# First units behind each norm multiply the residual before it is normed, with GpSimd taking part of the norm

## The reference

```
z = x @ w_in                                   # q, k, v of two attentions, forget logits, two gates
y = (sigmoid(ga) * (o_a @ w_pa) + sigmoid(gb) * (o_b @ w_pb)) @ w_o
x = layer_norm(ALPHA * x + y, ln1_g, ln1_b)    # norm 0 (layer 0), norm 2 (layer 1)
f = (gelu(conv3(x @ w_gate)) * (x @ w_up)) @ w_down
x = layer_norm(ALPHA * x + f, ln2_g, ln2_b)    # norm 1 (layer 0), norm 3 (layer 1, the output)

layer_norm(x, g, b) = (x - mean) * rsqrt(var + eps) * g + b
```

## Time and profile before

| | us |
|---|---|
| median of 3 runs (lowest, highest) | 960.76 (959.99, 963.42) |
| the profiled execution | 963.47 |
| its span, first to last instruction | 961.7 |
| TensorE busy in it | 936.3 (97%) |
| VectorE, ScalarE, GpSimd busy | 603.3, 506.5, 22.0 |

### The profile page before, as it was taken

The page is one execution under the profiler, slowest core; times in us unless marked ns, Lnnn a source line. Parts: engine busy times, 40 slices in busy tenths (PEclk is TensorE's granted clock), DMA queues, the critical chain, the costliest instruction groups (busy, mean ns, idle before and its releaser), DMA issues.

```text
span 961.7 us, 16399 instructions
## 1 busy us (share of the span) xinstructions
PE 936.3 (97%) x6488; PEld 900.9 (94%) x6488; DVE 603.3 (63%) x1211; ACT 506.5 (53%) x962; POOL 22.0 (2%) x39
## 2 busy tenths in 40 slices
PE   7999999998999999999899999999989999999996
PEld 5989999998999999999898999999989999999993
DVE  4675654678866666545587664548778566664545
ACT  4864454435855565533397544544467555653323
POOL 2000000000000000000000000000000000000000
PEclk9999999999999999999999999999989999999996
DMA  9744434554465554545735444355526555545511
GB/s 271 187 130 134 116 91 126 149 145 122 125 178 146 153 154 136 157 141 157 170 89 137 120 129 120 84 151 151 154 75 177 160 147 152 155 126 159 151 50 55
DMA packets 257765, 132.92 MB, mean 138 GB/s; under 512 B 22454, under 2 KB 254906, under 8 KB 257562
## 3 DMA queue, kind: packets, MB, share of 16 engines
q1 hardware_dynamic: 255930, 126.79, 47.4%
q0 software_dynamic: 1760, 5.09, 1.5%
HBM read 127.42 MB, written 4.57 MB: 137 GB/s over the span
## 4 chain that ended last, share of the span: by engine, by line
PE 97%; DVE 2%; ACT 1%; DMA 0%; issue 0%; SPq 0%; DVEq 0%
PE bank L625 28%; PE bank L626 27%; PE bank L627 27%; PE bank L695 3%; PE bank L840 2%; PE bank L641 1%; PE bank L647 1%; PE bank L644 1%; DVE roped_b L1394 1%; PE bank L799 1%; PE bank L795 1%; PE bank L792 1%; PE bank L814 1%; PE bank L696 1%; DMA gates<-in_x_sample 0%; DVE gates L1387 0%
## 5 line engine op out<-in xcount | busy, mean ns | idle before, releaser
L625 PE MATMUL bank<-act_hi,w_hi 128*128 128x320 f32 x1312 | 411.6, 314 | 0.0
L626 PE MATMUL bank<-act_lo,w_hi 128*128 128x320 f32 x1312 | 405.4, 309 | 0.0
L627 PE MATMUL bank<-act_hi,w_lo 128*128 128x320 f32 x1312 | 405.4, 309 | 0.0
L1161 DVE TENSOR_TENSOR w_lo<-raw,w_hi 128x1024 fp32r<-128x1024 f32 (+1 forms) x236 | 283.8, 1203 | 108.7 <-ACT w_hi L908 108.1
L908 ACT CAST w_hi<-raw 128x1024 fp32r<-128x1024 f32 (+1 forms) x236 | 244.2, 1035 | 154.7 <-PE bank L627 146.9
L625 PEld LDWEIGHTS bank<-act_hi,w_hi 128*128 128x128 f32 x1312 | 246.4, 188 | 2.7 <-DVE w_lo L1161 0.3
L626 PEld LDWEIGHTS bank<-act_lo,w_hi 128*128 128x128 f32 x1312 | 246.4, 188 | 0.2
L627 PEld LDWEIGHTS bank<-act_hi,w_lo 128*128 128x128 f32 x1312 | 246.3, 188 | 0.0
L625 PE MATMUL bank<-h_hi,w_hi 128*128 128x320 f32 x352 | 109.4, 311 | 0.0
L627 PE MATMUL bank<-h_hi,w_lo 128*128 128x320 f32 x352 | 108.8, 309 | 0.0
L626 PE MATMUL bank<-h_lo,w_hi 128*128 128x320 f32 x352 | 108.8, 309 | 0.0
(11 more groups left out here) (197 smaller groups left out, 999.3 us busy)
## 6 DMA issues: line engine op xcount, KB each, us to landing
raw<-in_w_in SPq DMA_DIRECT2D x62, 512.0 KB, 3.9
raw<-in_w_gate SPq DMA_DIRECT2D x44, 512.0 KB, 3.8
raw<-in_w_up SPq DMA_DIRECT2D x44, 512.0 KB, 4.3
raw<-in_w_down SPq DMA_DIRECT2D x32, 448.0 KB, 3.8
raw<-in_w_o SPq DMA_DIRECT2D x16, 512.0 KB, 4.1
raw<-in_w_down SPq DMA_DIRECT2D x16, 512.0 KB, 4.1
raw<-in_w_in SPq DMA_DIRECT2D x16, 256.0 KB, 5.2
raw<-in_w_pa SPq DMA_DIRECT2D x32, 128.0 KB, 2.8
```

What stands on the lines that cost most here:

```text
L625: pe.matmul(out, wh, hi[:, k0 + c, :], start=begin and c == 0, stop=False)
L626: pe.matmul(out, wh, lo[:, k0 + c, :], start=False, stop=False)
L627: mm = pe.matmul(out, wl, hi[:, k0 + c, :], start=False, stop=end and c == n_chunks - 1)
L1161: ve.tensor_tensor(w_lo[:, slot, :, :].rearrange("p c e -> p (c e)")[:, 0:w], raw[:, slot, 0:w], hi.bitcast(F32), ALU.subtract).then_inc(l ...
```

## The change

Norm of x times a weight is rewritten. With r the residual behind norm_tile (less its shift), W the weights and x = (r - mean) * root * g + b:

W x = root * (W (g r) - mean * (W g)) + W b

The first five units behind norms 0, 1 and 2 (FOLDED; gate 0, up 0, gate 1, up 1, gate 2, or forget, ka, va, qa 0, qa 1) multiply r_hi/r_lo, the two parts of g*r, with g and b as two more columns (322 in place of 320). r_hi is made by ACT and r_lo by DVE when a residual tile is ready. The statistics' matmuls stand within the first of these units. DVE then takes W g and W b from the bank (uv) and adds -mean * (W g) to the sum ("lift", into fixes, three buffers); GpSimd multiplies by the root and adds W b ("level"); the step behind reads fixes in place of the bank. GpSimd also centres all eight tiles and scales four of them. The three-unit group is gone: from the sixth unit on, units use act_hi/act_lo as before. The key transposes move to the units from ga 7 on, one tile behind each of five; cache and parameter transposes to units 2, 3 and 6 of their layer. The last norm is not folded, and there all centring comes behind the reciprocal. kT is split into kA and kB so that r_hi and r_lo have room.

```diff
-at_unit(TOP, "cache", 0)
-at_unit(TOP, "cache", 1)
-at_unit(TOP, "params", 0)
+at_unit(2, "cache", 0)
+at_unit(3, "cache", 1)
+at_unit(6, "params", 0)
...
-at_unit(NORM_UNITS[0], "keys", 0)
+for _k, _t in enumerate(KEY_TILES):
+    at_unit(AT[("ga", KC - 1)] + _k, "kv", _t)
...
+            def level(m, j):
+                at = FOLDED * m + j
+                pool.wait_ge(lifted, at + 1)
+                t = fixes[:, at % 3, :]
+                nc.gpsimd.tensor_tensor(t, t, rstd_of[m % 2], ALU.mult).then_inc(pool_chain, 1)
+                pool.wait_ge(pool_chain, at + 1)
+                nc.gpsimd.tensor_scalar(t, t, uv[:, j, 1:2], None, ALU.add).then_inc(levelled, 1)
+            def normalise(m):
...
+                passed(r_split, KC * (m + 1))
+                passed(mean_copied, m + 1)
+                for o in range(KC):
+                    nc.gpsimd.tensor_tensor(gates[:, o, :], gates[:, o, :], nmean_of[norm], ALU.add).then_inc(centred, 1)
+                passed(rstd_ready, m + 1)
+                level(m, 0)
+                for o in range(BY_POOL, KC):
+                    nc.gpsimd.tensor_tensor(gates[:, KC + o, :], gates[:, o, :], rstd_of[norm],
+                                            ALU.mult).then_inc(scaled_late, 1)
+                for j in range(1, FOLDED):
+                    level(m, j)
...
+                hi, lo, w = (r_hi[fold[0] % 2], r_lo[fold[0] % 2], WIDE) if fold else (act_hi, act_lo, TOK)
...
                 def ready(k):
-                    if fresh:
+                    if fold and fold[1] == 0:
+                        stats(fold[0], k)
+                        if k == 0:
+                            pe.wait_ge(edge_split, fold[0] + 1)
+                        pe.wait_ge(r_split, KC * fold[0] + k + 1)
+                    elif fresh:
                         pe.wait_ge(fresh[0], fresh[1](k))
...
+            def lift(l, u):
+                m, j = folding(l, u)
...
+                if j >= 3:
+                    dve.wait_ge(*consumed(l, u - 3))
+                dve.wait_ge(unit_used, SLOTS + unit_n(l, u + 1))
+                dve.wait_ge(mean_copied, m + 1)
+                b = bank[TILE[UNITS[u][:2]] % 4]
+                link(ve.tensor_copy(uv[:, j, :], b[:, TOK:WIDE]))
+                ve.scalar_tensor_tensor(fixes[:, at % 3, :], nmean_of[m % 2], uv[:, j, 0:1], b[:, 0:TOK], ALU.mult,
+                                        ALU.add).then_inc(lifted, 1)
...
+            def r_part(m, k):
...
+                dve.wait_ge(r_hi_made, KC * m + k + 1)
+                ve.scalar_tensor_tensor(r_lo[norm][:, k, 0:TOK], gates[:, k, :], par[:, g0 + k:g0 + k + 1],
+                                        r_hi[norm][:, k, 0:TOK].bitcast(F32), ALU.mult,
+                                        ALU.subtract).then_inc(r_split, 1)
...
+                    elif early == 1:
+                        lift(l, u)
+                        for o in (4, 5):
+                            lo(fold[0], o)
+                        lo_part(l, u + AHEAD + 1)
+                        for o in (6, 7):
+                            lo(fold[0], o)
+                        lift(l, u + 1)
+                    elif early in (2, 3):
+                        lift(l, u + 1)
```

More of the change, by code:

```diff
@@ L180 @@
 USES = []
-for _u in range(TOP, NU):
+for _u in range(NU):
     for _s, _i in SCHEDULE.get(_u, []):
@@ L192, with folding @@
 FROM_SHIFTED = 3
+FOLDED = 5
+BY_POOL = 4
+def folding(l, u):
+    g0 = AT[("gate", 0)]
+    if l > 0 and u < FOLDED:
+        return 2 * l - 1, u
+    return (2 * l, u - g0) if g0 <= u < g0 + FOLDED else None
 FIRST = KC
@@ L628, in products, with stats @@
                 return mm
[L630 to L650, removed]
+            def stats(m, k):
+                l, i = m // 2, m % 2
+                if k == 0:
+                    pe.wait_ge(added, n(l, (KC - 2) * (i + 1), 2 * (KC - 2)))
+                    pe.matmul(claim(l, ("mean", i))[:, 0:TOK], mean_w, sum_q, start=True, stop=False)
+                    pe.matmul(claim(l, ("square", i))[:, 0:TOK], mean_w, sum_sq, start=True, stop=False)
+                elif k == 3:
+                    pe.wait_ge(r_ready, n(l, KC * i + KC, 2 * KC))
+                    done(pe.matmul(bank[4 + USE[("mean", i)] % 4][:, 0:TOK], mean_w, gates[:, KC - 1, :], start=False,
+                                   stop=True))
+                elif k == 5:
+                    pe.wait_ge(squared, n(l, KC * i + KC, 2 * KC))
+                    done(pe.matmul(bank[4 + USE[("square", i)] % 4][:, 0:TOK], mean_w, gates[:, 2 * KC - 1, :],
+                                   start=False, stop=True))
             def unit(l, u):
@@ L856, in _ @@
             for l in range(DEPTH):
-                if l > 0:
-                    for kind, i in SCHEDULE[TOP]:
-                        step(l, kind, i)
-                    group(l, 0, GROUP)
-                else:
-                    for u in range(GROUP):
-                        unit(l, u)
-                    for kind, i in SCHEDULE[TOP]:
-                        step(l, kind, i)
                 for u in range(NU):
-                    if u == AT[("gate", 0)]:
-                        group(l, u, GROUP)
-                    elif UNITS[u] and u >= GROUP and not 0 < u - AT[("gate", 0)] < GROUP:
+                    if UNITS[u]:
                         unit(l, u)
@@ L1052, in step @@
                 elif kind == "norm":
+                    last = l == DEPTH - 1 and i == 1
+                    if not last:
+                        hi_part(*follow(l, i, 3))
                     b, v = spare(l, ("mean", i))
@@ L1095, in _, with follow @@
+            def follow(l, norm, k):
+                return (l, NORM_UNITS[0] + 1 + k) if norm == 0 else (l + 1, k)
             act.wait_ge(set_once, 6)
@@ L1239, in norm_tile @@
                                      ALU.add).then_inc(added, 1)
+                if norm == 0:
+                    for k in range(4) if o == 4 else (o - 1,) if o > 4 else ():
+                        r_part(2 * l, k)
+                    if o == KC - 1:
+                        edges(2 * l)
+                elif l < DEPTH - 1 and o == KC - 1:
+                    for k in range(4, KC - 1):
+                        r_part(2 * l + 1, k)
+                    edges(2 * l + 1)
                 b = tile_wait(l, (kind, o))
```

288 lines of the change are left out of this document (182 added, 106 removed).

## The result

The changed kernel takes 987.78 us (median of 4 runs, 987.33 to 989.36) against 962.09 (median of 4) for the kernel before: 1.0269 times as long, 95% interval 1.0245 to 1.0294. So it is slower by some 26 us; the forecast was no measurable change, 961.5, in a range of 949 to 975.

The account below looks back on a forecast made before the run. TensorE was taken as the bound, losing about 16.5 us behind three norms. Norm 0 +2.4, norm 1 -3.8, norm 2 +1.3 and end +0.8 gave +0.7 on 963.47, carried to the runs' median as 961.5; range 949 to 975.

Parts of the forecast that it names:

- What bounds the kernel, and the ceiling: TensorE holds 97% of the chain; about 16.5 us lost behind the three norms are the most to win.
- The start, 1.0 us late: Ahead of norm 0's statistics: DVE's remainders of the residual make TensorE start 1.0 us late, at 233.3.
- The walk: root, first normed tile, seventh unit: Queues behind norm 0: root at 241.3, first normed tile 243.5, seventh unit 260.9 against 262.20 before.
- ACT from there: Behind norm 0's first normed tile: 15 tile instructions at 0.56 us without waits, then copies and casts, ending at 259.2.
- GpSimd's price: 22 instructions a norm: 0.75 us for two inputs, 0.45 for one; bounds of 0.5 and 1.0 shift the seventh unit 0.4.
- The rival with slow GpSimd: At 1.25 us an instruction ACT waits for the levels: 3 us more at each norm, 970; chance 0.07.
- The rival of turns: Behind each norm GpSimd and DVE exclude each other: seventh unit about 4 us later, +12, 973.5; chance 0.32.
- Norm 1, -3.8 us: At norm 1 qa3 starts at 499.1 against 503.36, 4.3 us won, less 0.45 for uncovered parameter transposes.
- one of its own signs of being wrong: Time going anywhere outside the three norm stretches and the end was to show the prediction wrong.
- Moved key transposes, 1.64 us a layer: 15 key transposes moved out of the gap at norms 0 and 2 cost 1.64 us each time.
- the end, 0.8: At the last norm, centring behind the reciprocal puts two 0.40 us instructions before the first output transpose: +0.8.
- Norm 2: Same code as norm 0: 2.5 us won, 1.64 for transposes and 2.1 of clock lost, +1.3 in all.

Follow-up runs that it names:

- e1: The changed kernel with GpSimd's 22 instructions per norm on 8 of 320 columns, same waits and order; 969.05 us, 1.0063 times the kernel before.
- e5: The kernel of e1 with two memsets that nobody reads ahead of each 8-column GpSimd instruction; 981.63 us, 1.0190 times the kernel before.
- e4: The kernel before with five bursts of ten unused GpSimd instructions in layer 0, where GpSimd is otherwise idle; 964.44 us in one run.
- e9: The changed kernel with the root in a PSUM bank for DVE's four scales at norms 0 and 2; 984.29 us, 1.0240 times the kernel before.

## Why the prediction was wrong

- **What bounds the kernel, and the ceiling.** Right: the wait for normed tiles is gone, and all that came in its place is again time in which TensorE stands still or runs slowly.
- **The start, 1.0 us late.** Right: 1.14 and 1.15 us at norms 0 and 2.
- **The walk: root, first normed tile, seventh unit.** Right as far as GpSimd has no part: with the statistics 2.75 us later than assumed, the reciprocal ends at 244.05 in the changed kernel (241.3 + 2.75), and the seventh unit of e1 is at 263.36 (263.4; two errors of 0.8 and 0.6 us cancel there). Two small slips in the working change nothing: the clocks of the earlier trace rows are 0.63, 0.76 and 0.50, and the terms that lead to 256.6 add up to 256.3.
- **"ACT from there", with DVE's instructions at their lengths alone: the step that failed.** The forecast gave DVE 0.49 us for a scale or an act_lo and 1.14 for a remainder, and let ACT's 15 tile instructions follow each other without a wait; that DVE's lengths grow beside GpSimd stood only among the rivals. Measured in the changed kernel at norm 0: DVE's eleven instructions take 11.33 us and not 6.67, ACT waits 0.44, 0.91 and 0.99 us for scales, and its tiles end at 262.2, where the walk moved by 2.75 has 256.75. The remainder for the fifth unit, which the walk had ready, is late by the same row, and TensorE waits 3.06 us for it; the clock falls twice at norm 0 (6.0 us, not 2.1).
- **GpSimd's price: the term that was mis-sized.** 0.75 and 0.45 us were taken, with 0.5 to 1.0 as bounds. Measured: 1.04 and 1.42 on average in place, 0.87 and 1.08 at best. So 0.75 was near what two inputs take without DVE in the way, and 0.45 was far from what one takes: the cast that served as the nearest row has one input and eight times the elements, and taking it per element and per input made the one-input instruction the cheapest, while it is the dearest. A level, two instructions, takes 2.17 us and not 1.2. At 1.0 us an instruction the seventh unit was to come 0.8 us later than at 0.5; in e5, at 1.1 us a centring, it comes 2.8 later than in e1. The rival with slow GpSimd (ACT waits for the levels, 3 us at each norm, 7 in 100) was near that.
- **The rival of turns.** Its mechanism is real: DVE's scale beside GpSimd is over 0.7 us, as was asked of it, and e4, e5 and e9 show it apart. Its price at the seventh unit, about 4 us a norm, was near: DVE's row makes 4.7. It left out what comes besides, slower levels (1.6 us), the fifth unit's wait and a second fall of the clock. Price and turns had been set out as alternatives, and they came together, 20.5 us against e1: the range ended at 975 because no case had both.
- **Norm 1, -3.8 us.** Wrong apart from GpSimd too: e1 loses 1.0 there. The walk itself held and ended too soon, at qa3: that unit starts at 501.83 in e1, and 499.1 moved by the 2.62 us that e1 was late is 501.7 (before, 503.36 moved likewise is 506.0; 4 us won). But DVE and ACT have won next to nothing by then: their logf step, ahead of the scores, comes at 516.55, and 514.29 moved by 2.62 is 516.9. So TensorE gives back what it had won, in two waits for softened scores of layer 1's first heads, 1.63 and 1.88, and in the clock behind them (0.51 from 526.9 to 530.4). In the changed kernel these waits are 2.43 and 1.88. This is time outside the stretches that the prediction had named, one of its own signs of being wrong.
- **Moved key transposes, 1.64 us a layer; the end, 0.8.** Right: 1.64 and 1.63; 0.74.
- **Norm 2** follows norm 0: -0.3 us had been forecast (+1.3 less the 1.64 of transposes); e1 shows -0.9 and the changed kernel +6.1.

Left open is the division of the 20.5 us between slowness and turns. The two feed the same queues and each hides part of the other: without turns 13.4 remain (e5), on the way to the seventh unit turns make 4.7 of 6.2, and turns without slowness were not run.

## What to carry to other kernels

Giving part of a busy vector engine's work to GpSimd can lose, as here: 22 instructions of 0.4 us became 22 of about 0.8 to 1.5, others waited for them, and DVE's own eleven instructions beside them went from 6.7 to 11.3 us. So measure both first, GpSimd's time on that shape and DVE's beside it. When two engines share something, price both effects together and not as rivals, and put an operand in PSUM where the choice is free. Before folding a norm away to fill a gap, count what already fills it (the transposes were free there) and follow the engines' rows until they have caught up, not only to the first unit behind the gap.

## What the runs showed of the hardware

- A GpSimd instruction's time is hardly in its number of inputs: 320 columns took 1.20 us with two inputs (0.87 at best), 1.19 with one and a constant (1.01 at best) and 1.46 with one and a column of scalars (1.08 at best), all beside a busy DVE (e4); without an input (memset) 0.37, and 8 columns with two inputs 0.20 in eight of ten.
- Of two that meet, either can wait. Beside two-input GpSimd instructions DVE's two-input ones were up to 0.69 us longer, and GpSimd's own went up to 1.75; beside one-input ones GpSimd went up to 1.76 where 1.01 is its best, and DVE's 1.22 and 0.48 mostly stayed as they are (e4).
- A DVE instruction with one operand in PSUM did not wait: eight scales at 0.473 to 0.475 us, where four with both in SBUF had a median of 1.10 in the same kernel (e9).
- TensorE's granted clock is not a fixed price per wait: behind the wait of 3.06 us at norm 0 it read 0.50 for 3.6 us, behind the wait of 3.06 us at norm 2 it stayed at 1.00 (738.1 to 742.0).
